# Three early ring refills in quarters, and eight projection chunks placed behind later experts, in a two-block kernel on one core

## The reference, cut to what matters

```python
# first block, per expert e (top 4 of 32 experts per token)
h = xb @ w_gu[e] + b_gu[e]                      # 1024 -> 2048
g = jnp.minimum(h[:, ::2], 7.0)
lin = jnp.clip(h[:, 1::2], -7.0, 7.0)
a = g * jax.nn.sigmoid(1.702 * g) * (lin + 1.0)
y = a @ w_dn[e] + b_dn[e]                       # 1024 -> 1024
# second block, the memory projection
kv_me = rmsnorm_2(mem, norm_mem[l]) @ w_mem_kv[l]
```

## Time and profile before

| | before |
|---|---|
| median of 3 runs | 1636.64 us (1635.32 to 1637.49) |
| the profiled execution | 1635.43 us, its span 1633.6 us |
| PE busy | 1562.5 us, 96% of the span |
| PE weight loads / DVE / ACT busy | 57% / 34% / 27% |
| DMA | 526.55 MB, mean 322 GB/s |
| chain that ended last | PE 72%, DMA 19%, DVE 5%, ACT 2% |

### The profile page before, as it was taken

The page is one execution under the profiler, slowest core; times in us unless marked ns, Lnnn a source line. Parts: engine busy times, 40 slices in busy tenths (PEclk is TensorE's granted clock), DMA queues, the critical chain, the costliest instruction groups (busy, mean ns, idle before and its releaser), DMA issues.

```text
span 1633.6 us, 22540 instructions
## 1 busy us (share of the span) xinstructions
PE 1562.5 (96%) x9460; PEld 936.9 (57%) x9460; DVE 557.2 (34%) x1081; ACT 437.5 (27%) x885; POOL 25.2 (2%) x33
## 2 busy tenths in 40 slices
PE   6989899999999999999999999999899999999998
PEld 5876683434344343343333333333399988899986
DVE  3947541111111011121111101111245564468774
ACT  3435530111011011011101101110345563256553
POOL 0210000000000000000000000000000100000000
PEclk9999999999999999999999999999999999999999
DMA  9517578999999999999999999999935534434530
GB/s 387 210 52 310 225 287 336 435 422 434 427 432 432 428 433 429 431 430 432 431 431 434 431 431 433 430 433 431 421 153 176 178 123 157 162 148 163 199 129 26
DMA packets 28885, 526.55 MB, mean 322 GB/s; under 512 B 3092, under 2 KB 6292, under 8 KB 8293
## 3 DMA queue, kind: packets, MB, share of 16 engines
q1 hardware_dynamic: 25520, 520.51, 76.4%
q10 hardware_dynamic: 2772, 3.29, 0.8%
q0 software_dynamic: 512, 1.57, 0.4%
HBM read 524.28 MB, written 1.08 MB: 322 GB/s over the span
## 4 chain that ended last, share of the span: by engine, by line
PE 72%; DMA 19%; DVE 5%; ACT 2%; issue 1%; SPq 1%; POOL 0%; ACTq 0%; DVEq 0%; POOLq 0%
PE ps L669 70%; DMA ring<-in_w_down 15%; DMA ring<-in_w_gate_up 1%; DMA ring<-in_second 1%; DMA ring<-in_first 1%; PE ps L814 1%; SPq L587 0%; PE ps L1005 0%; ACT arena L1642 0%; DVE ring_r L1814 0%; PE ps L998 0%; PE ps L1213 0%; DVE mx L1931 0%; DVE arena L1892 0%; DMA small<-in_small 0%
## 5 line engine op out<-in xcount | busy, mean ns | idle before, releaser
L669 PE MATMUL ps<-ring,arena 128*64 128x512 f32 (+1 forms) x3840 | 707.0, 533 | 23.5 <-DMA ring<-in_w_down 14.1
L669 PEld LDWEIGHTS ps<-ring,arena 128*64 128x64 f32 (+1 forms) x3840 | 235.7, 132 | 440.4 <-issue 400.4
L669 PE MATMUL ps<-arena 128*128 128x128 f32 (+8 forms) x1732 | 302.4, 407 | 8.7 <-DVE arena L2072 1.7
L669 PEld LDWEIGHTS ps<-arena 128*128 128x128 f32 (+3 forms) x1732 | 174.7, 176 | 136.9 <-issue 121.3
L669 PE MATMUL ps<-arena_r,w_high 128*128 128x256 f32 x1360 | 247.8, 285 | 0.0
L2092 DVE TENSOR_SCALAR arena<-ps 128x512 f32<-128x512 f32 x32 | 22.1, 692 | 571.7 <-PE ps L669 571.7
L669 PEld LDWEIGHTS ps<-arena_r,w_high 128*128 128x128 f32 x1360 | 212.2, 192 | 2.9 <-issue 1.7
L669 PE MATMUL ps<-arena_r,ring_r 128*128 128x256 f32 x680 | 192.3, 283 | 0.0
L2175 DVE TENSOR_TENSOR ring_r<-ring,w_high 128x1024 fp32r<-128x1024 f32 x120 | 142.3, 1221 | 96.8 <-ACT w_high L1611 96.8
L1551 ACT ACTIVATE arena<-ps 128x256 f32<-128x256 f32 x32 | 12.3, 384 | 453.0 <-PE ps L998 453.0
L1611 ACT ACTIVATE w_high<-ring 128x1024 fp32r<-128x1024 f32 x120 | 121.3, 1053 | 37.7 <-PE ps L669 32.6
(11 more groups left out here) (222 smaller groups left out, 1075.1 us busy)
## 6 DMA issues: line engine op xcount, KB each, us to landing
ring<-in_w_gate_up SPq DMA_DIRECT2D x64, 4096.0 KB, 19.1
ring<-in_w_down SPq DMA_DIRECT2D x30, 4096.0 KB, 17.9
ring<-in_second SPq DMA_DIRECT2D x32, 2048.0 KB, 7.8
ring<-in_first SPq DMA_DIRECT2D x17, 2048.0 KB, 17.6
ring<-in_w_down SPq DMA_DIRECT2D x8, 1024.0 KB, 17.8
arena<-in_memory SPq DMA_DIRECT2D x4, 1024.0 KB, 10.1
ring<-in_first SPq DMA_DIRECT2D x4, 512.0 KB, 11.4
ring<-in_second SPq DMA_DIRECT2D x2, 1024.0 KB, 4.8
```

Of the source, the lines that this page charges most:

```text
L669: return nc.tensor.matmul(out_, lhsT, rhs, start=start, stop=stop, **kw)
```

## The change

- `EARLY_UNITS` (named, and otherwise unused) and a count `early_used` are added. The three `gate_up` calls of expert 0 (both halves) and expert 1 (first half) raise `early_used` after each of their first three quarters.
- `in_quarters` issues the first three refills (`w_gu[1, 1]`, `w_dn[0]`, `w_gu[2, 0]`) in four DMAs of 1 MB each, every quarter as soon as PE is through with the quarter of the buffer that it overwrites; before, they were three DMAs of 4 MB behind the whole use. PE waits for the three additional quarter semaphores where it first uses these refills.
- `CHUNKS_FROM` is 7. PE and ACT run experts 1 and 2 written out, 3 to 14 in a loop, and 15 to 30 written out, with the eight chunks behind experts 16, 18, ..., 30.
- SP's 1 MB of memory weights moves from ahead of step 6 to ahead of step 20.

```diff
--- before.py
+++ after.py
@@ -54,6 +54,7 @@
 PART = 1024
 HI_PARTS = SLOT // PART
 UNITS_EXPERT = 3
+EARLY_UNITS = 3
 SMALL = [("ident", 128), ("b_mod", 48), ("norm1_g", 8), ("cvec", 16)]
 SMALL_FIRST = sum(_width for _, _width in SMALL)
@@ -315,7 +316,8 @@
                                                       sem("gelu_set"), sem("f_set"))
         y_mm, o_set, o_out = sem("y_mm"), sem("o_set"), sem("o_out")
-        quarter_in = {(q, i): sem(f"quarter_in{q}{i}") for q in (1, 2) for i in range(3)}
+        early_used = sem("early_used")
+        quarter_in = {(q, i): sem(f"quarter_in{q}{i}") for q in range(3) for i in range(3)}
         gather_mm, x_ready, s_ready, sel_ready = sem("gather_mm"), sem("x_ready"), sem("s_ready"), sem("sel_ready")
         sg_ready, h_free, g_ready, sig_ready = sem("sg_ready"), sem("h_free"), sem("g_ready"), sem("sig_ready")
@@ -429,6 +431,7 @@
         N_CHUNKS = 8
+        CHUNKS_FROM = N_EXPERTS // 2 - 1 - N_CHUNKS
         def chunk(n):
@@ -557,12 +560,27 @@
                     sp.wait_ge(moe_units, e * UNITS_EXPERT)
                     pair_of(2, third, slot_full)
-                with sp.Fori(1, 6) as e:
+                def in_quarters(n, src):
+                    q = n % 3
+                    whole = ring[:, PAIRS[q]:PAIRS[q] + 2, :].rearrange("p a n -> p (a n)")
+                    for i in range(4):
+                        if i < 3:
+                            sp.wait_ge(early_used, 3 * n + i + 1)
+                        else:
+                            sp.wait_ge(moe_units, n + 1)
+                        at = slice(SLOT // 2 * i, SLOT // 2 * i + SLOT // 2)
+                        sp.dma_start(whole[:, at], src[:, at]).then_inc(
+                            quarter_in[q, i] if i < 3 else slot_full[PAIRS[q]], 16)
+                for n, src in enumerate((w_gu[1, 1], w_dn[0], w_gu[2, 0])):
+                    in_quarters(n, src)
+                with sp.Fori(2, 2 * CHUNKS_FROM + 6) as e:
                     step(e, w_gu[e + 1, 0])
                 sp.wait_ge(kv_mm, 2)
                 sp.wait_ge(kvw_in["v"], 16)
                 load_memory(3)
-                with sp.Fori(6, N_EXPERTS - 1) as e:
+                with sp.Fori(2 * CHUNKS_FROM + 6, N_EXPERTS - 1) as e:
                     step(e, w_gu[e + 1, 0])
                 sp.wait_ge(moe_units, (N_EXPERTS - 1) * UNITS_EXPERT - 2)
                 pair_of(0, w_gu[N_EXPERTS - 1, 1], slot_full)
@@ -963,7 +981,7 @@
                         at = 1024 * half + 512 * n
                         mm(ps[SLOTS * half:SLOTS * half + SLOTS, n, :], esel, b_gu[:, at:at + 512], True, False)
-            def gate_up(j, q, second_half):
+            def gate_up(j, q, second_half, signal=False):
                 w = wide(q, 4)
                 for kk in range(4):
@@ -973,6 +991,8 @@
                             at = 1024 * half + 512 * n
                             last = mm(ps[SLOTS * half:SLOTS * half + SLOTS, n, :], xg[:, k, SLOTS * j:SLOTS * j + SLOTS],
                                       w[:, kk, at:at + 512], False, k == KC - 1)
+                    if signal and kk < 3:
+                        last.then_inc(early_used, 1)
                 last.then_inc(moe_units, 1)
             def down(q, part, quarters=False):
@@ -981,7 +1001,7 @@
                 for f in range(4 * part, 4 * part + 4):
                     if quarters and f % 2 == 0:
                         if f < 6:
-                            pe.wait_ge(quarter_in[q, f // 2], 16)
+                            pe.wait_ge(quarter_in[q, f // 2], 32)
                         else:
                             pe.wait_ge(slot_full[PAIRS[q]], N_EXPERTS * 16 + 16 * fills1(PAIRS[q]))
                     for half in range(2):
@@ -1032,6 +1052,11 @@
             def round_pe():
+                def filled_early(n):
+                    for i in range(3):
+                        pe.wait_ge(quarter_in[n, i], 16)
                 def filled_pair(q, fills):
                     pe.wait_ge(slot_full[PAIRS[q]], fills * 16 + 16 * fills1(PAIRS[q]))
@@ -1054,15 +1079,19 @@
                         if done is not None:
                             last.then_inc(done, 1)
-                def body(e, j, pair, n=None, last=False):
+                def body(e, j, pair, n=None, last=False, early=()):
                     biases(e)
                     filled_pair(2, e)
-                    gate_up(j, 2, 0)
+                    if 2 in early:
+                        filled_early(2)
+                    gate_up(j, 2, 0, 0 in early)
                     combined(e - 2)
                     turn_gates(e - 1)
                     turn_hidden(e - 1)
                     filled_pair(0, e + 1)
+                    if 0 in early:
+                        filled_early(0)
                     gate_up(j, 0, 1)
                     pe.wait_ge(at_ready, e)
                     if pair is not None:
@@ -1071,6 +1100,8 @@
                     pe.wait_ge(sgt_ready, e + 1)
                     if not last:
                         filled_pair(1, e + 1)
+                    if 1 in early:
+                        filled_early(1)
                     down(1, 0, last)
                     if pair is not None:
                         gathered(pair, False)
@@ -1092,15 +1123,18 @@
                 biases(0)
                 gathered(0, True)
                 filled_pair(0, 1)
-                gate_up(0, 0, 0)
+                gate_up(0, 0, 0, True)
                 filled_pair(1, 1)
-                gate_up(0, 1, 1)
-                for i in range(N_CHUNKS):
-                    body(i * 2 + 1, 1, i + 1)
-                    body(i * 2 + 2, 0, None, i)
-                with pe.Fori(N_CHUNKS, N_EXPERTS // 2 - 1) as i:
+                gate_up(0, 1, 1, True)
+                body(1, 1, 1, early=(0, 1))
+                body(2, 0, None, early=(2,))
+                with pe.Fori(1, CHUNKS_FROM) as i:
                     body(i * 2 + 1, 1, i + 1)
                     body(i * 2 + 2, 0, None)
+                for n in range(N_CHUNKS):
+                    i = CHUNKS_FROM + n
+                    body(i * 2 + 1, 1, i + 1)
+                    body(i * 2 + 2, 0, None, n)
                 body(N_EXPERTS - 1, 1, None, last=True)
                 turn_hidden(N_EXPERTS - 1)
                 combined(N_EXPERTS - 2)
@@ -1584,12 +1618,15 @@
                 for half in range(2):
                     copy_gather(half, half + 1, 2 * SLOTS, 2 + half)
                 sigmoid(0)
-                for i in range(N_CHUNKS):
-                    body(i * 2 + 1, i + 1)
-                    body(i * 2 + 2, None, i)
-                with act.Fori(N_CHUNKS, N_EXPERTS // 2 - 1) as i:
+                body(1, 1)
+                body(2, None)
+                with act.Fori(1, CHUNKS_FROM) as i:
                     body(i * 2 + 1, i + 1)
                     body(i * 2 + 2, None)
+                for n in range(N_CHUNKS):
+                    i = CHUNKS_FROM + n
+                    body(i * 2 + 1, i + 1)
+                    body(i * 2 + 2, None, n)
                 body(N_EXPERTS - 1, None)
                 copy_hidden(N_EXPERTS - 1)
                 copy_gates(N_EXPERTS - 1)
```

## The result

| | before | after |
|---|---|---|
| median of 18 runs each | 1636.55 us | 1638.95 us |
| ratio, 95% interval | | 1.0018 (1.0011 to 1.0024) |
| the profiled execution | 1635.43 us, span 1633.6 | 1638.12 us, span 1636.2 |
| PE busy | 1562.5 us | 1562.9 us |

The changed kernel is 2.4 us slower (0.18%; by the interval 1.8 to 3.9 us). Between two of the 18 runs of the kernel before lie up to 5 us, and in the later sets up to 7. Two later runs, one of the kernel before with 3213.5 us and one of the experiments with 1847.9, are slow ones and in no interval. So I read the traces from a mark that all of them have: the first gate-up record of expert 0.

A forecast was written before the change was run, and what follows sets the result against it. Transfer landings were taken to set the experts' end, PE what follows. The tail's 1.8 us later last combination, with 1.7 us lead counted, gave +1.6 at the transposes: profiled 1637.0, median 1638.2, range 1634.0 to 1640.6.

The forecast's parts named there:

- What bounds the experts: Experts: landings of weight transfers set their end; PE's first-half work is hidden, so removing chunks from experts 2 to 16 gains nothing.
- What survives of the lead: First refills: of 5.5 us lead from quartering, 1.7 us are left at the sixth refill, bounds 0.5 to 1.9.
- the fifth: Fifth refill: issued at 294.89 with almost nothing in the queue, lands 12.3 us later at 307.2, not 308.9.
- the lower bound: Lead of at least 0.5 us: a transfer behind a restart took 10.9 us, not 9.7, costing the sixth refill 1.2.
- PE behind expert 20: Experts 20 to 30: down weight lands at 837.6, then PE sets the pace and is 0.75 us late at expert 30.
- The tail: Behind expert 30: the eighth chunk's 3.65 us are not fully hidden; next gate-up at 1142.25, last combination 1.8 us later.
- From the last combination to the transposes: `keep_warm` ends at 1185.7 after an unchanged 4.18 us idle, ACT's side at 1184.9; transposes at 1185.75, +1.6 us.
- The clock behind it: At the transposes behind the experts: 1.2 GHz (0.50) in both kernels, since the idle time ahead is the same.
- A: Second half: landings come later through 3.5 us of slow transfers, so PE is not late at expert 30; 1637.5; chance 0.22.
- B: First refills: the 5.5 us lead survives whole because the fourth refill finds a queue; 1634.4; chance 0.10.
- C: First refills: lead lost in queue restarts, sixth landing at or after 318.7; tail costs +3.35, 1640.0; chance 0.10.
- D: First refills: quarters served one by one, 4.8 us each instead of 2.43; sixth lands some 19 us late; 1656; chance 0.02.

The follow-up runs named there:

- the chunks alone: Kernel before with the changed kernel's chunk placement and memory weights at step 20, first refills still single 4 MB transfers: 1639.54 us, interval 1.0006 to 1.0025.
- nine refills in quarters: Changed kernel with chunks behind experts 14 to 28 and the first nine refills quartered, not three: 1635.34 us, interval 0.9985 to 1.0003 to the kernel before.
- the second trace: The changed kernel unaltered, traced again: 936.16 us from first gate-up record of expert 0 to the transposes; its repeat timing was 1638.19 us (1.0003 to 1.0021).
- One chunk alone: Kernel before with only its last chunk moved, from expert 16 to 30: 1638.22 us, interval 0.9998 to 1.0016.
- fillers: Changed kernel plus four unused matmuls in expert 20 ahead of the wait for its down weights: 1638.87 us, 1.0006 to 1.0023 to the kernel before.

## Why the prediction was right or wrong, point by point

- **What bounds the experts.** Right. The first half's PE work was hidden: landings take over the chain at 374.75. The chunks taken out there gained nothing, and the chunks alone were slower.
- **What survives of the lead.** The mechanism was right, the size wrong: 1.7 us forecast, 0.7 measured. The fourth refill went out at 283.80, 1.6 us before the last quarter ahead of it landed, and took 12.5 us, hardly more than the 12.3 forecast for an empty queue (12.1 to 13.7 in the six other traces with three quartered refills). The step that failed is the fifth. I let it go by the same row, 12.3 us, and it took 13.4 (13.3 to 13.5 in all seven). The queue had restarted for the fourth just before; the 1.1 us more are what the earlier trace rows show behind the other restart (10.9 for 9.7), which I had used for the lower bound and charged to the sixth. The third refill came in at 285.4 and not at 283.0: the first was 1.2 us later than I had it, and the next two took 9.9 and 10.7 us. That had hardly an effect, since the fourth took 12.5 us from its issue all the same. With nine refills in quarters the lead at the sixth was 2.9 to 3.8 us. This supports the place; that it is a cost of the restart itself, and not of something else at that time, was not tried apart.
- **PE behind expert 20.** The last landing in the chain was at 836.9 (837.6 forecast), PE was late for the down weight of expert 30 by 0.76 us (1130.86 against 1130.1; 0.75 forecast). That the two agree is partly chance: PE lost 1.42 us to a clock that I had not foreseen, and one refill, issued at 1004.48, landed 11.0 us and not 9.7 after the one ahead of it. In the second trace, at full clock, PE was late by 0.2.
- **The tail.** Right: 2.66 us at the first gate-up of expert 31, forecast 1.8 and the 1.0 of missing lead. One chunk alone gives 2.8.
- **From the last combination to the transposes.** The size is near, the path was wrong, and the sign that I had named for it, a `keep_warm` that ends after the diagonal is there, did not come. The 4.18 us ahead of it, which I took for fixed, are gone: it runs at 1180.23 right behind the last combination, and PE then idles 4.75 us for DVE. DVE scales the last down result at 1177.57 and only then subtracts the first weight parts (1178.71, in the chain), and the norm's product waits for that until 1180.99. Before, that subtraction was done beside PE's last combination, DVE then idled 0.5 us, and the product waited for ACT's first square until 1179.00. So the product slips by 1.99 us where PE and DVE slip by 2.6: of 2.6 us, 2.0 arrive. I had looked at ACT's side of this joint alone.
- **The clock behind it.** I had it the same in both. Its low stretch now reaches further into PE's work: four to six us behind the start of the transposes the granted clock was 0.91 before (window 1188 to 1190) and is 0.62 now (window 1190 to 1192), and the 40.40 us from the transposes to ACT's copy are 40.95. That is 0.55 of the 0.9 us by which +2.53 at that copy misses +1.6; the lead's 1.0, less the 0.6 that the joint took up, is the rest.
- **The rivals.** A (slow transfers fall into the later half) happened in part, once, for 1.3 us, and PE stayed late. B's condition nearly came, for the fourth refill did find 1.6 us of queue; its lead did not survive even so (12.5 us from issue to landing). C needed a sixth landing at or after 318.7; it was at 318.0, with 0.7 us of lead left. The median of 1638.95 lies 0.75 us above the forecast and 1.05 below C. D was refuted: quarters overlap, 10.0 us for four where one by one they would take 19.

## What to carry to other kernels

Work that fills gaps belongs where something behind it can still take it up. Here the same 3.65 us on PE cost nothing behind expert 16, where waits for landings followed in the second half, and 2.0 to 2.8 us to the transposes behind expert 30, where the next landings left only 0.91 us of idle time to fill. The other way round, a microsecond saved on PE is worth nothing once something else comes last at the next joint: look for the second-latest there. A lead at the start of a queue is worth only what the next issue that it doesn't speed up lets through: look for that issue before cutting transfers up. And when one or two per mille are the question, measure from a mark inside the trace too: here the times of one kernel spread by 5 us and more, the distances of one kernel by 1.

## What the runs showed that I had not expected

- **After a wait of under 3 us PE's clock fell in some traces and not in others.** Behind the first wait for a down weight among the late chunks (2.1 to 3.2 us, in nine traces without fillers) it fell to 0.50 in four: after waits of 2.72, 2.71, 2.52 and 2.08 us, and 16 records then took 5.07 to 5.35 us and not 3.65. It stayed at 1.00 in five, after 2.71, 2.71, 2.65, 3.19 and 2.10 us. So the length of the wait alone doesn't decide it, and one trace with a remedy proves nothing. The waits of 0.91 and 1.60 us of the kernel before brought it down in no trace.
- **The experts begin at different times in different runs of almost the same program ahead of them, in step with the clock.** The mark lies between 248.6 and 252.4 us, and the 13 traces form three groups by the granted clock from 230 to 239 and from 239 to 245: 0.81 and 1.00 in seven with marks from 248.6 to 249.9, 1.00 and 0.72 in four with marks from 250.6 to 251.3, 0.62 and 0.72 in two with 252.0 and 252.4. That, and the low clock behind the experts, are a good part of the 5 us between runs.
- **Slow transfers come in step.** In every trace two to six of the 4 MB transfers land 10.1 to 11.3 us after the one ahead of them and not 9.7, and most of these have a partner 205 to 218 us away: 439.5 and 645.0 in the kernel before, 815.0 and 1023.0 in the changed one. Nothing here names a cause.
- **The 4.18 us of PE ahead of `keep_warm` contain the fetch of an instruction block.** They are there (4.18, 4.32, 4.57) in the three kernels whose chunks, or all but one, stand early, and in none of the others. The queue that the profile calls "q8 instruction" moves blocks of 16 KB, and in the kernel before none from 780 to 1140, while PE's program loops. One such block starts between 1179 and 1180 in the kernel before, inside PE's wait (1177.7 to 1181.87); in the two others one starts inside the wait as well (between 1182 and 1183, and between 1181 and 1182). In the changed kernel none starts from 1176 to 1181; one did between 1173 and 1175. That fits a wait for program text behind the branch that stands ahead of `keep_warm`, but no run moves the block alone, so the cause is not shown. The line of that queue, in the DMA view of the kernel before from 1177.7 to 1181.87:

```profile
q8 instruction: 1, 0.02, 1.5%
```
